# The down weights of a mixture-of-experts loop on a second DMA queue

## What is computed

```python
logits = jnp.dot(h, w_router, preferred_element_type=jnp.float32) + b_router
top_v, top_e = lax.top_k(logits, TOP_K)          # 4 of 32 experts
gate = jax.nn.softmax(top_v, axis=-1)

gu = xe @ w_gu[e] + b_gu[e]                      # 1024 -> 2048
gt, up = jnp.split(gu, 2, axis=-1)
gt = jnp.minimum(gt, SWIGLU_LIMIT)
up = jnp.clip(up, -SWIGLU_LIMIT, SWIGLU_LIMIT)
act = gt * jax.nn.sigmoid(SWIGLU_ALPHA * gt) * (up + 1.0)
return act @ w_dn[e] + b_dn[e]                   # 1024 -> 1024
```

## Time and profile before

| | us |
|---|---|
| median of 3 runs | 1450.25 (1447.14 to 1451.82) |
| the profiled execution | 1445.29 |
| its span | 1443.5 |
| TensorE busy | 1302.7 (90%) |
| VectorE busy | 445.4 (31%) |
| ScalarE busy | 239.4 (17%) |
| GpSimd busy | 115.5 (8%) |
| packets of SP's queue, as a share of 16 DMA engines | 78.2% |
| moved on SP's queue | 463.81 MB |

### The profile page before, as it was taken

The page is one execution under the profiler, slowest core; times in us unless marked ns, Lnnn a source line. Parts: engine busy times, 40 slices in busy tenths (PEclk is TensorE's granted clock), DMA queues, the critical chain, the costliest instruction groups (busy, mean ns, idle before and its releaser), DMA issues.

```text
span 1443.5 us, 14072 instructions
## 1 busy us (share of the span) xinstructions
PE 1302.7 (90%) x5849; PEld 600.2 (42%) x5849; DVE 445.4 (31%) x771; ACT 239.4 (17%) x332; POOL 115.5 (8%) x140
## 2 busy tenths in 40 slices
PE   6999899999986999899999999999989988788772
PEld 4765677777562333333333333333333322223220
DVE  2697311111153242222222332222332422223325
ACT  3201343320011121111111111111111111111111
POOL 0110100000000011000000000010001011000010
PEclk9999999999977999999999999999999999899996
DMA  9614502633456899999999899999999999999995
GB/s 343 223 59 164 209 34 92 226 131 160 161 239 261 363 426 425 425 427 426 425 426 405 352 424 399 413 424 404 425 425 422 425 425 425 424 426 424 427 403 163
DMA packets 62332, 479.25 MB, mean 332 GB/s; under 512 B 11412, under 2 KB 11540, under 8 KB 37643
## 3 DMA queue, kind: packets, MB, share of 16 engines
q1 hardware_dynamic: 50975, 463.81, 78.2%
q0 software_dynamic: 9728, 10.53, 2.1%
q10 hardware_dynamic: 1516, 3.23, 0.7%
HBM read 479.54 MB, written 21.04 MB: 347 GB/s over the span
## 4 chain that ended last, share of the span: by engine, by line
PE 74%; DMA 18%; issue 3%; DVE 3%; ACT 2%; POOL 0%; SPq 0%; ACTq 0%; POOLq 0%; DVEq 0%
PE PS L1476 31%; PE PS L1202 15%; PE PS L1499 14%; DMA ring<-in_w_gu 9%; DMA arena<-in_w_gu 5%; PE PS L1148 5%; PE PS L1351 4%; DMA ring<-in_w_dn 2%; PE PS L1383 2%; PE PS L1226 2%; PE PS L1328 1%; DMA arena<-in_norm_mix 1%; DMA ring<-y_rows 0%; DMA y_rows<-arena 0%; PE PS L1280 0%
## 5 line engine op out<-in xcount | busy, mean ns | idle before, releaser
L1476 PE MATMUL PS<-ring,arena 128*64 128x512 f32 x1888 | 433.3, 613 | 47.7 <-issue 23.9
L1476 PEld LDWEIGHTS PS<-ring,arena 128*64 128x64 f32 x1888 | 139.9, 141 | 323.1 <-issue 284.7
L1069 DVE TENSOR_TENSOR arena<-PS,XN 128x1024 f32<-128x1024 f32 x32 | 39.2, 1225 | 695.6 <-PE PS L1476 695.6
L1202 PE MATMUL PS<-arena,ring 128*128 128x320 f32 x768 | 216.1, 440 | 0.5 <-ACT arena L557 0.5
L1499 PE MATMUL PS<-ring,arena 128*64 128x512 f32 x864 | 192.1, 596 | 9.3 <-DMA ring<-in_w_dn 9.3
L1202 PEld LDWEIGHTS PS<-arena,ring 128*128 128x128 f32 x768 | 147.1, 194 | 60.4 <-issue 3.2
L753 ACT ACTIVATE arena<-arena 128x1024 f32<-128x1024 f32 x32 | 33.9, 1058 | 683.7 <-DVE arena L1072 683.7
L1476 PE MATMUL PS<-arena 128*64 128x512 f32 x544 | 125.5, 612 | 16.2 <-issue 8.5
L493 POOL DMA_INDIRECT y_rows<-arena x64 | 64.7, 1011 | 856.4 <-ACT arena L747 826.9
L1499 PEld LDWEIGHTS PS<-ring,arena 128*64 128x64 f32 x864 | 59.2, 137 | 126.0 <-issue 108.7
L1148 PE MATMUL PS<-ident,arena 128*128 128x128 f32 (+4 forms) x607 | 87.3, 286 | 15.3 <-DVE arena L1083 6.2
(11 more groups left out here) (176 smaller groups left out, 697.8 us busy)
## 6 DMA issues: line engine op xcount, KB each, us to landing
ring<-in_w_gu SPq DMA_DIRECT2D x98, 2048.0 KB, 19.4
ring<-in_w_dn SPq DMA_DIRECT2D x46, 2048.0 KB, 19.5
arena<-in_w_gu SPq DMA_DIRECT2D x30, 2048.0 KB, 19.4
arena<-in_w_dn SPq DMA_DIRECT2D x18, 2048.0 KB, 25.5
ring<-in_w_in SPq DMA_DIRECT2D x12, 2048.0 KB, 11.9
ring<-in_w_mem_kv SPq DMA_DIRECT2D x2, 2048.0 KB, 21.7
ring<-in_cache_mem_k SPq DMA_DIRECT2D x4, 1024.0 KB, 13.3
ring<-in_cache_mem_v SPq DMA_DIRECT2D x4, 1024.0 KB, 15.0
```

Source lines behind the costliest of these rows:

```text
L1069: nc.vector.tensor_tensor(gbuf[:], PS[:, 0:2, :], g_bias, ALU.add).then_inc(sems["g_added"], 1)
L1202: last = mm(PS[:, j % 2, 0:T], w[:, k, m * P:(m + 1) * P], hT[:, k, :], start=k == 0, stop=k == KT - 1)
L1476: last = mm(PS[64 * h:64 * h + 64, 2 * g + b, :], xT[:, k, b * BLK:(b + 1) * BLK], moe_ring(m, 2)[:, kk, g * D + h * 512:g * D + (h + 1) * ...
```

## The change

The helper `expert_chunk` takes the queue that issues as an argument. SP issues the first eight chunks as before, and then the gate/up chunks alone. In ScalarE's loop, step e begins with a wait for `gu_done` of expert e; behind it ScalarE issues the two chunks of down e. The two of down 31 are issued in step 30 instead, behind `move_out(29)`, since their slots are those of down 29. The slots, the semaphores on which TensorE waits and the order of TensorE's work stay.

```diff
--- before.py
+++ after.py
@@ -305,6 +305,12 @@
         m = AT[(NE - 1, r)]
         return moe_ring(m, 4)[:, 0:TT, :]
 
+    def expert_chunk(queue, m):
+        e, c = STREAM[m]
+        if c < 4:
+            return queue.dma_start(moe_ring(m, 2), wgu[e, :, 2 * c:2 * c + 2, :])
+        return queue.dma_start(moe_ring(m, 4), wdn[e, c - 4])
+
     normfin = moe_ring(AT[(NE - 1, 0)], 4)[:, TT, :]
     bdn = XN[:, 0, :]
 
@@ -370,12 +376,6 @@
                 sp.dma_start(X[:, 0:2, :], x_p).then_inc(x_again, 16)
                 sp.dma_start(X[0:ROWS[2], 2, :], x_s).then_inc(x_again, 16)
 
-        def expert_chunk(m):
-            e, c = STREAM[m]
-            if c < 4:
-                return sp.dma_start(moe_ring(m, 2), wgu[e, :, 2 * c:2 * c + 2, :])
-            return sp.dma_start(moe_ring(m, 4), wdn[e, c - 4])
-
         def free(sems, v, m):
             name, per_window, count = consumed(m)
             sp.wait_ge(sems[name], per_window * v + count)
@@ -386,7 +386,7 @@
             else:
                 sp.wait_ge(y_done, 24)
                 sp.wait_ge(merged_ready, 16)
-            expert_chunk(m).then_inc(moe_loaded(m), 16)
+            expert_chunk(sp, m).then_inc(moe_loaded(m), 16)
 
 
         sp.wait_ge(cnt_ready, 1)
@@ -399,10 +399,10 @@
                     sp.wait_ge(moe_loaded(m), moe_arrived(m))
                 else:
                     sp.wait_ge(over_back, 16 * RING * (w - 1))
-                expert_chunk(m).then_inc(over_loaded[m % RING], 16)
+                expert_chunk(sp, m).then_inc(over_loaded[m % RING], 16)
             sp.wait_ge(over["dn_done"], NE * w)
             for m in range(RING):
-                expert_chunk(m).then_inc(over_back, 16)
+                expert_chunk(sp, m).then_inc(over_back, 16)
 
         with sp.If(most > WIN):
             over_stream(1)
@@ -413,8 +413,9 @@
         sp.nop()
 
         for m in range(RING, NCH):
-            free(main, 0, m - RING)
-            expert_chunk(m).then_inc(moe_loaded(m), 16)
+            if STREAM[m][1] < 4:
+                free(main, 0, m - RING)
+                expert_chunk(sp, m).then_inc(moe_loaded(m), 16)
 
 
         sp.wait_ge(main["gu_done"], NE)
@@ -749,6 +750,12 @@
         def window(sems, v):
             move_tokens(sems, v, 0)
             for e in range(NE):
+                if sems is main:
+                    act.wait_ge(main["gu_done"], e + 1)
+                    for m in () if e == NE - 1 else (AT[(e, 4)], AT[(e, 5)]):
+                        if e == 0:
+                            act.wait_ge(main["chunk_used"], m - RING + 1)
+                        expert_chunk(act, m).then_inc(moe_loaded(m), 16)
                 act.wait_ge(sems["g_ready"], NE * v + e + 1)
                 nc.scalar.activation(sbuf[:], gbuf[:], ACT.Sigmoid, scale=ALPHA).then_inc(sems["sig_done"], 1)
                 if e + 1 < NE:
@@ -758,6 +765,9 @@
                     nc.scalar.activation(GT[0:NE, :], PS[0:NE, 7, 0:T], ACT.Copy).then_inc(gt_ready, 1)
                 if e >= 1:
                     move_out(sems, v, e - 1)
+                if sems is main and e == NE - 2:
+                    for m in (AT[(NE - 1, 4)], AT[(NE - 1, 5)]):
+                        expert_chunk(act, m).then_inc(moe_loaded(m), 16)
                 act.wait_ge(sems["ta_done"], NE * v + e + 1)
                 nc.scalar.activation(actT[:].rearrange("p b j t -> p b (j t)"), PS[:, 6:8, :], ACT.Copy) \
                     .then_inc(sems["actT_ready"], 1)
```

## The result

The changed kernel takes 1471.57 us (median of 4 runs, 1467.15 to 1471.95) against 1448.7 us for the kernel before on the same chip: a ratio of 1.0159, interval 1.0127 to 1.0191. Slower by 23 us.

What follows compares the result with a forecast made beforehand. Weight transfers at 425 GB/s were taken to set the loop's time. Terms 0 + 3 + 5 + 13 + 2 = 23 us on the profiled 1445.3 gave 1468, then 1473 us as it lay 5 us under the median; range 1456 to 1489.

Steps and rivals of the forecast that it cites:

- (a) ScalarE's issues cost nothing: ScalarE's loop: two issues, 0.7 us, fit before the sigmoid 3.3 us after gate/up: 0; uncovered, 24 us.
- (c) Equal shares: DMA engines: two weight queues share equally, packet by packet, 9.86 us a chunk on each queue.
- (c) Start, 5 us: First experts: down chunks beside gate/up delay gate/up 5 by 5 us, bounds 0 and 10 (two chunks), carried over in full.
- (c) End, 13 us: Loop's end: tail grows 13 us (bounds 0, 19) by arrival order; in brackets: clock at 0.5 changes it within 0.5 us.
- fourth rival: Worse: ScalarE's queue gets more than half, or the low clock lasts through the tail's down products: 1491 us, chance 10%.
- (b) Late issue, 3 us in the middle: Dry stretches of the queue: the first down chunk issued one chunk of work later costs 3 us, bounds 0 and 9.8.
- (d) Longer code loads, 2 us: TensorE's "issue" gaps in the middle, read as code loads, grow by 2 us beside another queue, bounds 0 and 11.
- the faster one: First rival: two queues in flight fill the DMA engines better; 1428 us at 5% more rate, chance 4%.
- the one without a change: Second rival: TensorE's slack takes all and the tail's order does not matter; 1452 us, chance 8%.
- the one with service by time of issue: Third rival: chunks served by time of issue across queues, no term at the end; 1457 us, chance 10%.
- The rival of step 3 that late issue is the whole cost: Follow-up rival: issuing down chunks behind the gate/up product costs everything; 1471 us for late issue alone; no chance given.
- that ScalarE's issues are it: Follow-up rival: the issues and the wait on ScalarE cost; 1.015 with experts 30, 31 back on SP; no chance given.

Runs made afterwards that it cites:

- e5: The changed kernel without its delay: ScalarE issues each down chunk once the slot it fills is free; two queues stay: 1467.48 us, 1.0143 of before.
- e4: The kernel before, SP's queue alone, with both down chunks of an expert waiting for the end of its gate/up product: 1458.49 us, 1.0070 of before.
- e1: The changed kernel with the down chunks of experts 30 and 31 back on SP's queue in the old order: 1464.23 us, 1.0111 of before.
- e8: The changed kernel with the down chunks of experts 26 to 31 back on SP's queue: 1460.59 us, 1.0079 of before.
- e2: The changed kernel with the down chunks of experts 0 to 4 back on SP's queue in the old order: 1464.66 us, 1.0111 of before.
- e6: The changed kernel with 48 more matmuls on TensorE ahead of the last gate/up chunk of expert 31: 1480.45 us, 1.0214 of before.
- e7: The kernel before, SP's queue alone, with expert 1's gate/up product cut in two and expert 0's activation turn between: 1445.77 us, 0.9992 of before.
- e10: The changed kernel with only the down chunks of experts 5 to 25 on ScalarE's queue, all others on SP: 1456.1 us, 1.0061 of before.
- e11: The changed kernel with only experts 5 to 25 on ScalarE's queue, each down chunk issued once its slot is free: 1450.76 us, 1.0019 of before.
- e3: The changed kernel with the down chunks of experts 0 to 4 and 30, 31 back on SP's queue: 1456.53 us, 1.0070 of before.

## Why the prediction was right, point by point

The forecast was 1473 us and slower; 1471.6 us were measured, for the stated reasons in the main. That the number came so close is partly luck: the terms for start and end were both too small, and what hid it lies outside them (see "Sum").

- **(a) ScalarE's issues cost nothing: right.** 0.82 us for two, hidden in the 3.1 us until the sigmoid.
- **(c) Equal shares: right.** The last gate/up chunks come 9.85 us apart. The Trainium skill ("DMA: Bandwidth & Descriptors", section "Queues, rings and completion order") has the engines go round their queues by packets, and this trace agrees. That the second queue is the main cause is shown by e5 against e4; that it acts by the order of arrival, by the landings in the traces and by e1 and e8, where the old order gives the tail back. No run had the new order on one queue.
- **(c) Start, 5 us: too small.** Gate/up 5 started 10.7 us late, just above the bound of two chunks. I counted 20 weight chunks and nothing beside them. From 451.3 to 556.6 us the queue of GpSimd's gathers and scatters took 3.2% of the engines' time, 3.4 us, and 0.7 MB of the next expert's first chunk had moved ahead of the last of gate/up 4, 1.6 us. The slow product that I had allowed for was there (5.47 us) and cost nothing, as the next chunk was later still. That a lag here "carries over in full" was the weaker step: by e2 6 of the 11 us do at most.
- **(c) End, 13 us: right in mechanism, measured 17.7.** The last gate/up chunk landed 7.3 us ahead of the last weight, where I had 5.8. The mis-sized step is the clock. By the sentence in brackets a slow product ahead of the tail changes nothing, as both ends move alike; but gate/up 30's last product took 3.65 us, and only products within the tail were slow. e6 puts their part at 6 us, which leaves some 12 us for order. 3.2 of the 6, in the last bias sum and down 31, are what my fourth rival had in part, and e7 shows them without a second queue. e2 and e5, which don't have them, still have tails of 19.9 and 21.9 us.
- **(b) Late issue, 3 us in the middle: too small by itself.** e10 against e11 gives 0.4%, 5 to 6 us, with intervals that all but touch. In the changed kernel only 2.8 us more lag arise between experts 5 and 20, since its TensorE is late already and runs into fewer free moments. I had also missed a new dry stretch at large expert 7 (272 and 230 GB/s from 660 to 680 us) and the depth of the one at 900 us.
- **(d) Longer code loads, 2 us: about right.** "Issue" waits from 564 to 1133 us went from 22.7 to 24.7 us. That these gaps are loads of code was only a reading when I wrote it, and the traces bear it out. In the kernel before all six gaps over 1.5 us in this stretch hold one packet of the queue that the page calls "instruction", and TensorE goes on 2 to 3 us behind it; there are 44 such packets in 569 us, so chance would put 2 in the 21.4 us of those gaps. The gap of 5.31 us before 1057.00 us, its packet (count, MB, share of the 16 engines):

```profile
q8 instruction: 1, 0.02, 1.3%
```

In the changed kernel the packet lies in five of seven such gaps and just ahead of the other two. Whether the second queue made the gaps longer, 2.0 us in all, is not shown.
- **Sum.** In the profiled executions 15.7 + 17.7 us came in place of 10 + 13, 10 us more than forecast. Against them stand 3.3 us that I had not counted, behind the loop, and 4.0 us ahead of it that are no effect of the change; that leaves 26. The medians differ by 23. So the direction, the main term and the places are as forecast; the agreement to a microsecond is not earned by the terms.

Of the rivals, the faster one falls with 425 GB/s in the part bound by transfers, the one without a change and the one with service by time of issue fall with the shares and the tail. The rival of step 3 that late issue is the whole cost falls with e5; that ScalarE's issues are it falls with e1, e3 and e8, which leave 25 or more of the 32 pairs on ScalarE and still differ by their ends, and with e11, which leaves 21 and costs 0.2%.

No version beat the kernel before. e11 and e7 can't be told from it.

## What to carry to other kernels

Here, where transfers set the time, a second queue gave no bandwidth (425 GB/s with one or two); it changed the order of arrival, and weights that were needed next then shared the engines with weights needed later. Look at what such an order does at the two ends: behind the last landing there should be only the work of the last chunk, and putting the last two items back in order is not enough when the consumer has fallen behind over many. Tie an issue to the use of the very slot it fills, not to a later event, above all where the queue runs dry.

## What the runs showed of the hardware

Between 700 and 1330 us GpSimd's scatters and gathers took longer to land beside two weight queues than beside one. The changed kernel, then the kernel before (count, median us to landing):

```profile
y_rows<-arena POOLq DMA_INDIRECT x40, 11.2
arena<-h_rows,arena POOLq DMA_INDIRECT x20, 18.0
```

```profile
y_rows<-arena POOLq DMA_INDIRECT x42, 8.9
arena<-h_rows,arena POOLq DMA_INDIRECT x21, 14.0
```

11.2 instead of 8.9 us and 18.0 instead of 14.0 us: the small transfers slow down beside a third user of the engines, though TensorE's waits show none for them. What I had not expected is how much the clock of TensorE adds. A wait for weights of 6.2 us was followed by a product of 6.53 us for 3.65 at a granted clock of 0.50, and behind the wait of 1.11 us for ScalarE's copy the last down product took 9.36 us in the changed kernel, 9.38 in e1 and 9.29 in e8, but 7.09 in the kernel before and in e6. e7 has 9.28 with one queue, e2 and e5 have 7.09 with two. The difference in what TensorE did before is not plain: in e8 and e7 it had waited at most 1.9 us at a time over the last 80 us, as in the kernel before, and in e1 not at all for weights since 1386 us. This stays open.
